# First-layer attention scores as three products of q and k in parts, and the vs columns made in two more mixed pairs

## The reference, cut to what matters

```python
def first_block(x, norm_mix, w_in, att_rel_bias, sgu_norm_gain, ...):
    xn = rmsnorm(h, norm_mix[l])
    proj = xn @ w_in[l]
    q, k, v, u, vs, gate_logits = jnp.split(proj, ...)   # 512, 512, 512, 512, 512, 2048 columns
    att = chunked_rel_attention(q, k, v, att_rel_bias[l])
    sgu = spatial_gating(jax.nn.gelu(u), jax.nn.gelu(vs), sgu_norm_gain[l], sgu_norm_bias[l], ...)
    gates = jax.nn.sigmoid(gate_logits.reshape(B, S, N_BRANCHES, D) + b_gate[l])
    merged = gates[:, :, 0] * (att @ w_br_att[l]) + gates[:, :, 1] * (sgu @ w_br_sgu[l])
    h = h + merged @ w_out[l]
...
def chunked_rel_attention(q, k, v, rel_bias):            # 8 heads of 64, chunks of 64 tokens, 8 to the left
    scores = jnp.einsum('bcqhd,bckhd->bhcqk', qc, kb).astype(jnp.float32) * (Dh ** -0.5)
    probs = jax.nn.softmax(scores + bias, axis=-1)
    out = jnp.einsum('bhcqk,bckhd->bcqhd', probs, vb)
...
def spatial_gating(u, v, ln_g, ln_b, w_s, b_s):
    v = layernorm(v, ln_g, ln_b)
    mixed = jnp.einsum('gts,bnsgd->bntgd', w, vg) + b_s.T[...]
    return u * mixed.reshape(B, S, SGU_WIDTH)
```

## Time and profile before

| | us |
|---|---|
| median of 3 runs | 3275.19 |
| lowest, highest | 3275.11, 3275.71 |
| the profiled execution's own time | 3276.46 |
| its span in the profile | 3274.7 |
| TensorE busy | 3155.5 (96%) |
| VectorE / ScalarE / GpSimd busy | 2077.0 / 1217.4 / 1640.7 |

### The profile page before, as it was taken

One profiled execution on the slowest core, in us unless ns is written; L12 is line 12 of the kernel. 1 busy time (PEld: TensorE's weight loads), 2 busy tenths in 40 slices (PEclk: granted clock), 3 DMA queues, 4 the chain that ended last, 5 costly groups with the idle time before them and its releaser, 6 DMA issues.

```text
span 3274.7 us, 41085 instructions
## 1 busy us (share of the span) xinstructions
PE 3155.5 (96%) x15100; PEld 2503.7 (76%) x15100; DVE 2077.0 (63%) x2453; ACT 1217.4 (37%) x2029; POOL 1640.7 (50%) x966
## 2 busy tenths in 40 slices
PE   8999999999999999989999999999999999999998
PEld 6776678777888888878876667888878868777776
DVE  6336645787555577887865665333457768988826
ACT  5335521033333344532324443333344441333342
POOL 5771134337888855313322137888884433333333
PEclk9999999999999999999999999999999999999999
DMA  3232114112232286322211113232247611111112
GB/s 123 103 109 70 42 55 180 51 39 74 100 118 105 83 282 203 105 76 74 64 38 36 38 71 109 96 109 96 96 176 227 194 59 33 50 44 44 44 39 71
DMA packets 99472, 305.12 MB, mean 93 GB/s; under 512 B 11280, under 2 KB 11920, under 8 KB 98832
## 3 DMA queue, kind: packets, MB, share of 16 engines
q1 hardware_dynamic: 86976, 250.39, 23.1%
q10 hardware_dynamic: 12368, 53.00, 4.3%
HBM read 243.57 MB, written 59.77 MB: 93 GB/s over the span
## 4 chain that ended last, share of the span: by engine, by line
PE 68%; POOL 11%; DVE 9%; issue 7%; ACT 3%; DMA 1%; ACTq 0%; POOLq 0%; DVEq 0%; SPq 0%
PE acc L537 23%; PE acc L1620 14%; PE acc L1691 13%; POOL w_lo L3799 7%; PE acc L557 5%; PE acc L1004 2%; PE acc L978 2%; PE acc L3315 2%; PE acc L581 2%; DVE conv_slots L3207 1%; PE acc L631 1%; POOL raw L3794 1%; POOL gate_columns L3794 1%; PE acc L955 1%; ACT band_probs L1119 1%
## 5 line engine op out<-in xcount | busy, mean ns | idle before, releaser
L3784 POOL TENSOR_TENSOR w_hi<-raw,zero 128x1024 fp32r<-128x1024 f32 x105 | 214.6, 2044 | 1136.3 <-PE acc L537 503.2
L3788 POOL TENSOR_TENSOR w_lo<-raw,w_hi 128x1024 fp32r<-128x1024 f32 x112 | 313.9, 2803 | 108.7 <-ACT w_hi L2599 100.4
L3799 POOL TENSOR_TENSOR w_lo<-raw,w_hi 128x512 fp32r<-128x512 f32 x186 | 300.1, 1629 | 88.8 <-ACT w_hi L1728 88.7
L1620 PE MATMUL acc<-x_hi,w_hi 128*128 128x512 f32 x812 | 318.9, 393 | 7.2 <-DVE act_g L2134 3.6
L1620 PE MATMUL acc<-x_lo,w_hi 128*128 128x512 f32 x812 | 317.1, 391 | 0.0
L1620 PE MATMUL acc<-x_hi,w_lo 128*128 128x512 f32 x812 | 317.0, 390 | 0.0
L537 PE MATMUL acc<-x_hi,w_hi 128*128 128x512 f32 x816 | 255.7, 395 | 9.9 <-POOL w_lo L3788 4.5
L1620 PE MATMUL acc<-t_hi,w_hi 128*128 128x512 f32 x672 | 262.5, 391 | 2.7 <-POOL w_lo L3799 1.5
L1620 PE MATMUL acc<-t_lo,w_hi 128*128 128x512 f32 x672 | 261.9, 390 | 0.0
L1620 PE MATMUL acc<-t_hi,w_lo 128*128 128x512 f32 x672 | 261.8, 390 | 0.0
L537 PE MATMUL acc<-x_lo,w_hi 128*128 128x512 f32 x816 | 252.2, 391 | 0.0
(11 more groups left out here) (522 smaller groups left out, 7041.5 us busy)
## 6 DMA issues: line engine op xcount, KB each, us to landing
raw<-blocks SPq DMA_DIRECT2D x121, 512.0 KB, 3.6
part<-hid_dram SPq DMA_DIRECT2D x137, 256.0 KB, 3.6
raw<-row_pieces SPq DMA_DIRECT2D x44, 512.0 KB, 3.7
piece_block<-row_pieces SPq DMA_DIRECT2D x44, 512.0 KB, 3.8
hid_dram<-hidden_sums SPq DMA_DIRECT2D x22, 768.0 KB, 5.8
raw<-column_stack SPq DMA_DIRECT2D x22, 512.0 KB, 5.7
raw<-column_stack SPq DMA_DIRECT2D x44, 256.0 KB, 5.3
gate_columns<-column_stack SPq DMA_DIRECT2D x22, 512.0 KB, 3.6
```

What stands on the lines that cost most here:

```text
L1620: ins = pe.matmul(bank, half_tile(w, at_, k), part[:, k, :], start=(begins and k == 0 and m == 0), stop=(k == QUARTER - 1 and m == 2), ski ...
L3784: pool.tensor_tensor(hi, raw[:, slot, :], nothing, ALU.add).then_inc(hi_split, 1)
L3788: pool.tensor_tensor(lo, raw[:, slot, :], hi.bitcast(F32), ALU.subtract).then_inc(w_split, 1)
L3799: pool.tensor_tensor(half_tile_range(w_lo, at_), halves(source), half_tile_range(w_hi, at_).bitcast(F32), ALU.subtract).then_inc(half_spli ...
```

## The change

1. **Scores.** Each score is three fp32r products (q_hi k_hi, q_lo k_hi, q_hi k_lo) instead of one float32 product. For units 1 to 3, ScalarE copies high_hi and low_hi and VectorE subtracts high_lo and low_lo within the early pairs; four tiles are stored where two were, and four are loaded. For unit 0 both engines split q and k right behind k's scaling, and TensorE waits for it (qk_lowered).
2. **vs tiles.** EARLY_PAIRS grows from 9 to 11: the four vs tiles are made in two mixed pairs, with Gelu on ScalarE and four stores to vs_dram. One DMA of 2 MB, issued in the last attention unit, brings them back. The SGU turns all four in a row; the block in the last unit is now the first u tile.
3. **SGU layer norm.** Two operations a row instead of three; the first u tile is taken ahead of the statistics.
4. **Last PLE pair.** ScalarE takes steps 2 and 3 ahead of low_gate(4), VectorE lower_part 2 and 3 ahead of the multiplication of ple_high.
5. Some semaphores are merged, buffers are placed anew, and the stream of weights follows the new order.

```diff
-EARLY_PAIRS = GATE_PAIRS + HEAD_PAIRS - 1
+QK_PAIRS = HEAD_PAIRS - 1
+EARLY_PAIRS = GATE_PAIRS + QK_PAIRS + 2
...
-                    for side in range(2):
-                        ins = pe.matmul(acc[slots[side]][:, c0:c1], a.q_t[rows_of(side), p * P:(p + 1) * P],
-                                        a.k_t[rows_of(side), first + c0:first + c1], start=True, stop=True)
-                        if c1 == count:
-                            ins.then_inc(acc_full[slots[side]], 1)
+                    for m, (q, k) in enumerate(((band_q_hi, band_k_hi), (band_q_lo, band_k_hi), (band_q_hi, band_k_lo))):
+                        for side in range(2):
+                            ins = pe.matmul(acc[slots[side]][:, c0:c1], q[rows_of(side), p * P:(p + 1) * P],
+                                            k[rows_of(side), first + c0:first + c1], start=(m == 0), stop=(m == 2))
...
             def high(i):
                 act.wait_ge(high_scaled, i + 1)
+                if GATE_PAIRS <= i < GATE_PAIRS + QK_PAIRS:
...
+                    act.activation(high_hi[:, :], act_g[:, :], ACT.Copy).then_inc(qk_rounded, 1)
+                    return
                 if i >= GATE_PAIRS:
-                    act.dma_start(qk_dram[:, 2 * (i - GATE_PAIRS), :], act_g[:, :]).then_inc(high_out, 16)
+                    act.activation(act_g[:, :], act_g[:, :], ACT.Gelu_apprx_tanh).then_inc(early_made, 1)
+                    await_own()
+                    act.dma_start(vs_dram[:, 2 * (i - GATE_PAIRS - QK_PAIRS), :], act_g[:, :]).then_inc(high_out, 16)
                     return
...
             def low(i):
                 act.wait_ge(low_scaled, i + 1)
+                if GATE_PAIRS <= i < GATE_PAIRS + QK_PAIRS:
+                    n = i - GATE_PAIRS
+                    if n:
+                        act.wait_ge(low_out, stores_before(i))
+                    act.activation(low_hi[:, :], low_gate[:, :], ACT.Copy).then_inc(qk_rounded, 1)
+                    act.wait_ge(qk_rounded, 2 * n + 2)
+                    act.wait_ge(qk_lowered, 2 * n + 2)
+                    for half, (hi, lo, out) in enumerate(((high_hi, high_lo, high_out), (low_hi, low_lo, low_out))):
+                        act.dma_start(qk_dram[:, 2 * n + half, 0, :], hi[:, :].bitcast(F32)).then_inc(out, 16)
+                        act.dma_start(qk_dram[:, 2 * n + half, 1, :], lo[:, :].bitcast(F32)).then_inc(out, 16)
+                    return
...
                 dve.tensor_tensor(low_gate[:, :], snaps[:, :], rstd[:, :], ALU.mult).then_inc(low_scaled, 1)
+                if GATE_PAIRS <= i < GATE_PAIRS + QK_PAIRS:
+                    rounded = 2 * (i - GATE_PAIRS)
+                    dve.wait_ge(qk_rounded, rounded + 1)
+                    dve.tensor_tensor(high_lo[:, :], act_g[:, :], high_hi[:, :].bitcast(F32), ALU.subtract).then_inc(qk_lowered, 1)
+                    dve.wait_ge(qk_rounded, rounded + 2)
+                    dve.tensor_tensor(low_lo[:, :], low_gate[:, :], low_hi[:, :].bitcast(F32), ALU.subtract).then_inc(qk_lowered, 1)
...
         def sgu_tensor(pe, t):
-            for pair in range(2):
-                if pair:
-                    feature_block(pe, t)
-                    feature_block(pe, t)
-                for q in range(2):
-                    pe.wait_ge(vs_gelu, t.next("vs_gelu"))
-                    turn_tiles(pe, t, vs_t[:, q, :])
-            with t.loop(2, acc0=1, acc1=1, block=2):
-                feature_block(pe, t)
+            pe.wait_ge(vs_back, 16)
+            for j in range(SGU_TILES):
+                turn_tiles(pe, t, vs_early[:, j, :])
+            for _ in range(SGU_TILES - 1):
                 feature_block(pe, t)
```

## The result

The changed kernel takes 3291.01 us (median of 5 runs, 3288.82 to 3292.23) against 3275.24 us for the kernel before on the same chips: ratio 1.0049, interval 1.0036 to 1.0062. It is 15.8 us slower. The prediction was 3283.7 with a range from 3270.0 to 3291.0: the direction was right, the loss was nearly twice what the sum gave (+8.5), and the median lies a hundredth of a microsecond outside the range.

What follows compares the result with a forecast made beforehand. TensorE, busy in 96% of the span, bounds the kernel through its matmuls and pauses. Terms -5.4, +11.1, +5.4, +0.7, +2.5, +0.5, -0.8, -2.5, -3.0 sum to +8.5 on 3275.2: 3283.7 us, range 3270 to 3291.

Steps and rivals of the forecast that it cites:

- Rivals B and A: Pairs behind q/k pairs: B, low half stays hidden, 3268.7 us, chance 0.14; A, 2.3 us stalls, clock stays, 3274.1, 0.22.
- The size of the stall: Product 2 in three pairs behind q/k pairs: TensorE stalls 3.7 us each, +11.1 us in all (6.9 to 13.5).
- The clock: Behind the three stalls TensorE drops to its lower clock, 1.8 us lost each, +5.4 us (0 if stalls stay under 2.5).
- The clock at the start of the attention: Around unit 0's first score: a small clock fall, +0.5 us (0 to 0.9).
- The k split: Before unit 0's first score: two more instructions of the split delay it, +2.5 us (2.3 to 3.0).
- The attention: Score rounds, mostly set by VectorE and ScalarE: faster scores gain in eight places, -0.8 us (-2.4 to 0).
- Rival C: Attention scores: the two sides' fp32r products don't run side by side, +9 us on top, near 3292.7 us, chance 0.12.
- VectorE against GpSimd: Subtractions behind q/k pairs: 1.23 us alone, 2.31 beside GpSimd; by the skill's rule both slowed, the upper end, 13.5 us.
- The pairs for the blocks: vs tiles: four plain blocks (43.5 us) become two mixed pairs (38.1 us) on TensorE, -5.4 us.
- the SGU: Behind the attention: two waits for the Gelu of vs go, 3.1 us; ScalarE's copies pace the turns, +0.6; -2.5 us.
- the first vs pair: Early pairs: Gelu stands where the gate's sigmoid stood, with a table load in ScalarE's wait, +0.7 us.
- The last PLE pair: Row steps: 2.1 us off TensorE's idle and half a chance the 1.8 us clock fall goes, -3.0 us (-3.8 to -0.2).

Runs made afterwards that it cites:

- experiment 1: Changed kernel with ScalarE's low half of each q/k pair (copy, wait for the subtractions, four stores) moved behind the next pair's first snapshot: 3275.36 us.
- experiment 2: Changed kernel with float32 scores again, without the split, extra stores and extra loads; the rest of the change kept: 3264.14 us, ratio 0.9968 to the kernel before.
- experiment 4: Changed kernel with two stores (512 KB and 1.5 MB) instead of four behind each q/k pair, same bytes: 3282.88 us, one run.
- experiment 6: Changed kernel with q/k stores and loads of units 1 to 3 cut to half the bytes, same number of DMAs: 3289.55 us, one run.
- experiment 9: Changed kernel with 17 filler matmuls ahead of product 2 in the three pairs behind a q/k pair: 3286.21 us.
- experiment 3: Changed kernel with 15 filler matmuls ahead of TensorE's wait for unit 0's q and k split: 3288.63 us.
- experiment 5: Changed kernel with only the q_hi by k_hi product in each score; splits, stores, loads and waits kept: 3288.95 us.
- experiment 7: Changed kernel with the low half behind the snapshot, two stores for four, and fillers ahead of unit 0's split wait: 3271.91 us.

## Why the prediction came out at half of the loss

- **What bounds the kernel, and which step turns the sign: right.** TensorE's pauses set the time. The stall of product 2 behind low_hi, two subtractions and four starts came at the predicted place, in three pairs, released by snaps; experiment 1 removes it and experiment 2 shows the time without part 1 of the change. Rivals B and A, a chain that stays hidden or short stalls, fall: the idle is 4.44 us each time.
- **The size of the stall: mis-sized, put at 3.7 us and measured at 4.6.** The part on VectorE was right: one subtraction slowed to 2.32 us and one at 1.21, so that low_lo ended at 208.83, or 210.53 by the clock of the prediction (the pair starts 1.70 us earlier), between its 209.44 and 211.60. The step that failed is "an issue takes 0.48 us where several stand in a row". The earlier trace rows has that price for two loads that follow one another; the four stores took 0.33, 0.46, 0.81 and 1.21 us, from the first start to w_hi 2.93 us where 1.82 stood in the sum. Three times 1.1 us more would have given +14.4 instead of +11.1, against 13.8 measured. Experiment 4 takes the third and fourth start away and experiment 6 halves their bytes; the idle shrinks by 2.1 us in the one and by 0.9 to 1.1 in the other.
- **The clock: right in kind, mis-sized by its length.** The prediction priced each fall at 1.8 us, from one idle of 3.39 us before steady work. Behind the stalls it was 7.0 us for three, of which fillers give back 5.6 (experiment 9). The step that failed is "for about 3.4 us" behind each of the six idles. The trace of before doesn't bear that out: behind its two longest, 5.23 us at 1471.7 and 4.38 at 1934.1, the lower clock lasted 4.1 and 5.9 us, and the stalls that were forecast, 2.3 to 4.5 us, reach up to that. Nor is 2.50 us a bound: the same trace has a seventh fall at 1854.7, behind idles of 1.99 and 1.19 us. Its window behind the idle of 4.38 us:

```profile
1934.10:1940.00 5.90, 5.90 (x14) 4.64 (x15) 5.83 (x5) 4.38 (x4) 0.00 (x0) 0.50 0.23 79
```

- **The clock at the start of the attention: the largest single miss.** "A small clock fall, 0 to 0.9" was priced at 0.5. The idle was put at 2.9 us and was 3.76, and the clock stayed at the lower level for 12.9 us behind it; experiment 3 shows that this cost 3.5 us. Its size was partly chance: behind the same idle and the same work it lasted 3.4 us in experiment 1, which costs about 1.3 us (42.13 against 40.85). What decides the length stays open.
- **The k split: +3.6 instead of +2.5.** The chain is k's scaling, ScalarE's copy behind it (315.21), and the subtraction; the fillers, put behind the wait by the change, come on top of it. I took the subtractions and didn't count the fillers that now follow the wait.
- **The attention: right.** The rounds are set by VectorE's and ScalarE's loop; -0.4 against -0.8. Experiment 5 shows what cheaper scores can bring, 0.6 us a unit. The stretch from the first score to the last v block, though, grew from 163.2 to 165.2 us, which the prediction had named as a sign of being wrong; the growth is all in unit 0, at the lower clock. Rival C falls: the two sides' fp32r products run side by side. In the trace after the change (start us, us, both sides in one row as x2) the next pair of 512 columns starts 0.23 us behind this one, the time of a single product:

```profile
343.62 0.40 PE L980 MATMUL acc<-band_k_hi,band_q_lo 64*128 64x512 f32 x2
343.85 0.41 PE L980 MATMUL acc<-band_k_lo,band_q_hi 64*128 64x512 f32 x2
```

- **The rule on tiles of the array.** The Trainium skill's "TensorEngine Tiling (Array Packing)", "Key Properties", lets different tiles load and multiply in parallel and makes no exception for a type; the rows above, two fp32r products of 512 columns in 0.23 us, agree with it.
- **VectorE against GpSimd.** One of the two subtractions was slowed, high_lo at 2.32 us, and not both. The Trainium skill's "SBUF — State Buffer", "Who interferes with whom", has the one issued first decide; the trace agrees with the lock, but the use made of it in the prediction (both slowed) was wrong, since GpSimd's two instructions, from 203.08, were over by 206.61, before low_lo started at 207.62.
- **The pairs for the blocks, the SGU, the first vs pair: right** within 0.3 us.
- **The last PLE pair: half.** The idle shrank by 1.1 us, the wait that was removed; GpSimd still slowed three of VectorE's instructions to 2.3 us. The step that failed is "its later instructions meet one or two of GpSimd's fewer". The half chance that the clock's fall goes was not unsound: it stayed in the changed kernel, behind 2.28 us of idle, but in experiments 1 and 7 idles of 2.20 and 2.03 us had no lower clock behind them, and the 300 matmuls took 70.48 and 70.28 us, the predicted 3 us less than before.
- **The range** ended at 3291.0. The upper bounds of the stalls (13.5) and of the clock (5.4) with the other terms as they stood give 3286; the price of a start and the length of a clock fall had no upper bound of their own, each being one row's value. In the profiled execution the forecast's loss was as near to the measured one as it was only because stretches that the change doesn't touch gave back 3.4 us.

## What to carry to other kernels

Ahead of a wait that TensorE has behind a slower engine, count each instruction that an edit puts in, its DMA starts too; three extra starts and two subtractions here cost more than the whole rest of the change gained. A matmul form that is cheaper on TensorE is worth only what the rounds leave to TensorE: try the form with work left out first (one product instead of three gave 0.6 us a unit) before paying for its operands. Where an idle of some microseconds can't be removed, filling it can keep the lower clock away: that gave 5.6 us over three idles here.

## What the runs showed of the hardware that was not expected

- **A DMA start has no fixed price.** Four stores of 512 KB in a row took 0.33, 0.46, 0.81 and 1.21 us to start on ScalarE, the same in each of three pairs; with 256 KB each 0.33, 0.46, 0.47 and 0.47; two stores, of 512 KB and 1.5 MB, 0.33 and 0.46. So it isn't the size of the store being started alone (1.5 MB started in 0.46), nor the number of starts alone. The first store of 512 KB landed 2.6 us after its start, so it was still in work when the third and the fourth were started. But four loads of 512 KB in a row in the attention took 0.45 us each in one unit, one of them 0.91 in the next and 0.63 in the third, so bytes in work don't settle it either; the cause stays open.
- **The lower clock behind an idle lasts for different times.** Behind three idles of about 4.4 us it lasted 4.6, 6.1 and 3.4 us; behind 3.76 us at one and the same place 12.9, 3.4, 5.1, 9.9 and 12.4 us in five kernels with the same code there (the changed kernel and experiments 1, 9, 6 and 4); behind 2.35 us it fell in two pairs and not in the third (experiment 4). In the three pairs it cost half of its time, 7.0 of 14.1 us; at the start of the attention, where TensorE is not always what the others wait for, 3.5 of 12.9. Fillers in the idle kept it away (experiments 3 and 9). It also fell in lighter work with no idle above 0.72 us ahead of it (experiment 5).
